# Fetching and weighing the other experts' rows inside the last expert's steps

## The reference

```python
def moe_swiglu(h, router_w, w1, w3, w2):
    t = h.reshape(-1, shp[-1])
    logits = (t @ router_w).astype(jnp.float32)
    top_v, top_i = lax.top_k(logits, TOP_K)                  # TOP_K = 2
    top_w = jax.nn.softmax(top_v, axis=-1)
    gates = jnp.sum(jax.nn.one_hot(top_i, N_EXPERTS) * top_w[..., None], axis=1)
    y = jnp.zeros_like(t)
    for e in range(N_EXPERTS):                               # 8 experts, 3584 wide
        y = y + gates[:, e:e + 1] * swiglu(t, w1[e], w3[e], w2[e])
...
x_lat = x_lat + ms[5] * rmsnorm(y_lat, post_ffn_g[l])
```

## Time and profile before

| | |
|---|---|
| median of three runs | 1730.58 us |
| the profiled execution, its own time | 1729.34 us |
| its span, first to last instruction | 1727.5 us |
| TensorE busy | 1694.0 us, 98% |
| DVE busy | 1405.9 us, 81% |
| ACT busy | 1095.6 us, 63% |
| POOL busy | 84.2 us, 5% |
| granted TensorE clock, mean | 0.999 |

### The profile page before, as it was taken

How to read it: one execution, slowest core, us unless ns; L and a number is a source line. 1 busy time by engine, 2 the same in 40 slices (tenths; PEclk the granted TensorE clock), 3 DMA queues, 4 the chain that set the end, 5 groups by cost and what they waited for, 6 DMA issues and landing times.

```text
span 1727.5 us, 24198 instructions
## 1 busy us (share of the span) xinstructions
PE 1694.0 (98%) x7988; PEld 1373.9 (80%) x7988; DVE 1405.9 (81%) x1625; ACT 1095.6 (63%) x1403; POOL 84.2 (5%) x97
## 2 busy tenths in 40 slices
PE   7999999999999999999999999999999999999997
PEld 4876878888788877787888888888888888888885
DVE  4947677375664589879999999999999999999998
ACT  5435462222222354777788888888888888888886
POOL 0114000000010010300100000000000000000001
PEclk9999999999999999999999999999999999999999
DMA  9858826264475358369999999999999999999995
GB/s 344 293 183 293 286 89 197 90 191 132 149 232 165 119 93 299 119 237 351 378 397 395 395 388 394 370 380 393 358 395 388 362 396 376 375 395 369 383 377 189
DMA packets 229696, 506.05 MB, mean 293 GB/s; under 512 B 16304, under 2 KB 47152, under 8 KB 229344
## 3 DMA queue, kind: packets, MB, share of 16 engines
q1 hardware_dynamic: 225296, 493.04, 80.0%
q0 software_dynamic: 4320, 12.00, 2.4%
HBM read 498.12 MB, written 19.96 MB: 300 GB/s over the span
## 4 chain that ended last, share of the span: by engine, by line
PE 92%; DVE 4%; issue 1%; ACT 1%; DMA 1%; SPq 0%; DVEq 0%; ACTq 0%
PE ps L661 29%; PE ps L663 28%; PE ps L662 28%; PE ps L1203 1%; DVE w_lo L1742 1%; PE ps L918 1%; PE ps L953 1%; DMA raw<-in_ada_w 1%; PE ps L941 0%; PE ps L688 0%; PE ps L1169 0%; PE ps L708 0%; PE ps L770 0%; DMA xs<-in_x 0%; PE ps L681 0%
## 5 line engine op out<-in xcount | busy, mean ns | idle before, releaser
L1742 DVE TENSOR_TENSOR w_lo<-raw,w_hi 128x1024 fp32r<-128x1024 f32 x570 | 684.1, 1224 | 163.7 <-ACT w_hi L1279 136.9
L1653 ACT ACTIVATE w_hi<-raw 128x1024 fp32r<-128x1024 f32 x448 | 473.0, 1061 | 103.0 <-PE ps L663 102.7
L661 PE MATMUL ps<-w_hi,he_hi 128*128 128x512 f32 x896 | 353.9, 395 | 0.7 <-DVE w_lo L1742 0.6
L663 PE MATMUL ps<-w_hi,he_lo 128*128 128x512 f32 x896 | 349.5, 390 | 0.0
L662 PE MATMUL ps<-w_lo,he_hi 128*128 128x512 f32 x896 | 348.9, 389 | 0.0
L1742 DVE TENSOR_TENSOR w_lo<-raw_more,w_hi 128x1024 fp32r<-128x1024 f32 x224 | 273.2, 1225 | 29.5 <-ACT w_hi L1653 12.0
L1653 ACT ACTIVATE w_hi<-raw_more 128x1024 fp32r<-128x1024 f32 x224 | 237.7, 1062 | 49.5 <-PE ps L663 49.5
L1279 ACT ACTIVATE w_hi<-raw 128x1024 fp32r<-128x1024 f32 x122 | 128.3, 1059 | 206.0 <-PE ps L663 185.4
L663 PEld LDWEIGHTS ps<-w_hi,he_lo 128*128 128x128 f32 x896 | 168.2, 188 | 35.8
L661 PEld LDWEIGHTS ps<-w_hi,he_hi 128*128 128x128 f32 x896 | 168.2, 188 | 35.3 <-DVE w_lo L1742 1.6
L662 PEld LDWEIGHTS ps<-w_lo,he_hi 128*128 128x128 f32 x896 | 168.4, 188 | 33.6
(11 more groups left out here) (304 smaller groups left out, 1956.4 us busy)
## 6 DMA issues: line engine op xcount, KB each, us to landing
raw<-in_moe_w SPq DMA_DIRECT2D x448, 512.0 KB, 6.4
raw_more<-in_moe_w SPq DMA_DIRECT2D x224, 512.0 KB, 6.5
raw<-in_ada_w SPq DMA_DIRECT2D x96, 512.0 KB, 4.8
raw<-in_ffn_w SPq DMA_DIRECT2D x66, 512.0 KB, 4.4
raw<-in_w_in SPq DMA_DIRECT2D x40, 512.0 KB, 6.6
raw<-in_w_out SPq DMA_DIRECT2D x16, 512.0 KB, 5.9
yrows<-in_x SPq DMA_DIRECT2D x9, 512.0 KB, 16.8
xe<-xrows SPq DMA_DIRECT2D x7, 512.0 KB, 6.6
```

Of the source, the lines that this page charges most:

```text
L661: pe.matmul(o, lh, rh, start=start, stop=False)
L663: return pe.matmul(o, ll, rh, start=False, stop=stop)
L1653: act.activation(w_hi[:, s % SPL, :], expert_raw(i), ACT.Copy).then_inc(hi_done, 1)
L1742: dve.tensor_tensor(w_lo[:, s_ % SPL, :], src, w_hi[:, s_ % SPL, :].bitcast(F32), ALU.subtract)\
```

## The change

Four things change.

- POOL no longer waits for the landing of unit 83 of the last expert but for that of unit 26 (`FETCH_AT`), then for `y kept`, and gathers the four pieces ahead of its branch. In the branch, if it is taken, it gathers them again.
- DVE weighs and sums one piece in each of steps 3 to 6 of the last expert (`SUM_STEP`), behind `ae32` and ahead of the next `w_lo`: (tb 0, j 0), (tb 0, j 1), (tb 1, j 0), (tb 1, j 1). Each waits for both gathers of its block, and DVE waits for its end before it goes on.
- Behind the branch the weighing is gone; in the branch it is done anew from the second gather.
- The four semaphores of the gathers become two, one for each block.

```diff
+FETCH_AT = 26
+SUM_STEP = 3
...
-            landed, count = expert_in(UE - 1)
+            def fetch_rows():
+
+                for tb in range(NLAT):
+                    for j in range(2):
+                        pool.indirect_dma_start(ygot[:, tb, j, :], None, yrows[:, :],
+                                                bass.IndirectOffsetOnAxis(ap=dest[:, NLAT * j + tb:NLAT * j + tb + 1], axis=0))\
+                            .then_inc(sg("y got%d" % tb), 16)
+
+            landed, count = expert_in(FETCH_AT)
             pool.wait_ge(landed, count + (NE - 1) * (16 * UE // RAW_E))
             pool.wait_ge(sg("y kept"), 16 * (NE - 1))
+            fetch_rows()
             with pool.If(busiest > P):
                 pool.wait_ge(sg("y kept"), 32 * NE)
-            for tb in range(NLAT):
-                for j in range(2):
...
+                fetch_rows()
...
+            def weigh_rows(tb, j, count):
+
+                dve.wait_ge(sg("y got%d" % tb), 2 * count)
+                gate = rs[:, 4 + 2 * j + tb:5 + 2 * j + tb]
+                if j == 0:
+                    ins = dve.tensor_scalar(yout[:, tb, :], ygot[:, tb, 0, :], gate, None, ALU.mult)
+                else:
+                    ins = dve.scalar_tensor_tensor(out=yout[:, tb, :], in0=ygot[:, tb, 1, :], scalar=gate, in1=yout[:, tb, :],
+                                                   op0=ALU.mult, op1=ALU.add)
+                ins.then_inc(sg("y summed"), 1)
+                dve.wait_ge(sg("y summed"), 4 * (count // 16 - 1) + 2 * tb + j + 1)
...
                         dve.tensor_tensor(ae32[:, s % 2, :], sge[:, s % 2, :], ps[:, 2 * (s % 2) + 1, :], ALU.mult)\
                             .then_inc(sg("ae32"), 1)
+                        if last and turn == 0 and s >= SUM_STEP:
+                            weigh_rows((s - SUM_STEP) // 2, (s - SUM_STEP) % 2, 16)
                         if s:
                             split_to(end_w2(s - 1) + AHEAD - (s == STEPS - 1))
...
             with dve.If(busiest[0] > P):
                 experts(1)
-            def sum_rows(tb):
...
+                for tb in range(NLAT):
+                    for j in range(2):
+                        weigh_rows(tb, j, 32)
...
-            sum_rows(0)
-            sum_rows(1)
             add_last(0)
             add_last(1)
```

More of the change, by code:

```diff
@@ L645, in _ @@
             busiest = pool.value_load(flag[0:1, 0:1], min_val=0, max_val=NLAT * P)
-            landed, count = expert_in(UE - 1)
+            def fetch_rows():
[5 more added lines that the diff above has]
+            landed, count = expert_in(FETCH_AT)
             pool.wait_ge(landed, count + (NE - 1) * (16 * UE // RAW_E))
             pool.wait_ge(sg("y kept"), 16 * (NE - 1))
+            fetch_rows()
             with pool.If(busiest > P):
                 pool.wait_ge(sg("y kept"), 32 * NE)
-            for tb in range(NLAT):
-                for j in range(2):
-                    pool.indirect_dma_start(ygot[:, tb, j, :], None, yrows[:, :],
-                                            bass.IndirectOffsetOnAxis(ap=dest[:, NLAT * j + tb:NLAT * j + tb + 1], axis=0))\
-                        .then_inc(sg("y got%d%d" % (tb, j)), 16)
+                fetch_rows()
         @block.tensor
```

## The result

| | kernel before | changed kernel |
|---|---|---|
| median, 20 runs each | 1729.32 us | 1732.13 us |
| from the lowest to the highest | 1728.62 to 1731.64 | 1730.08 to 1733.27 |
| the profiled execution, its own time | 1729.34 | 1732.18 |
| its span | 1727.5 | 1730.4 |

The ratio of the changed kernel to the one before is 1.0013, 95% interval 1.0007 to 1.0019. The median lies 0.7 us above the 1731.4 that was forecast, inside the range. The median of the kernel before, over 20 runs, is 1.3 us lower than the three runs had shown, so the difference of the medians is 2.8 us where 0.8 was forecast. It is smaller than the 0.2% (3.5 us) that the prediction asked of a measurement; but the interval lies wholly above 1, so with 20 runs of each kernel a small loss can be told.

The account below looks back on a forecast made before the run. TensorE was taken to set the pace. Span 1727.5 + 0.35 + 1.12 - 0.67 = 1728.3 us, 0.80 more; on the 1730.58 median that gives 1731.4 us, range 1728.8 to 1733.8.

Parts of the forecast that it names:

- The room of DVE: Last expert: weighing behind ae32 costs nothing in steps 3 and 5, 0.35 us in step 4, 1.12 in step 6.
- all hidden: Rival, 17%: in the last expert TensorE loses nothing and only the end's 0.67 us is won; 1729.9 us.
- less room: Rival, 12%: in the last expert all four weighing operations cost TensorE, 0.3 us more at each; 1732.6 us.
- The fetch costs nothing: Gather behind unit 26: weights land in at most 12.7 us, within the 14.5 allowed, so 0 us.
- The backlog: DMA queues behind the moved fetch: colliding transfers add 5.4 us to the 7.3 us landing of weights.
- starves the weights: Rival, 6%: the fetch makes ACT's w_hi 3.6 us late from about 1633 us, felt fully by TensorE; 1735.0 us.
- The exclusive lock: Shared DVE and GpSimd ports: a w_lo could stand still while POOL issues; as a rival 1%, 1735.6 us.
- The end gains 0.67 us: Behind the branch: without the weighing the fourth addition starts at 1718.07 instead of 1718.74, gaining 0.67 us.
- The sum: Whole kernel: losses of 0.35 and 1.12 us less the 0.67 gain, 0.80 us more; forecast 1731.4 us, 61%.

Follow-up runs that it names:

- sum_step2: Changed kernel with DVE's four weighing operations in steps 2 to 5 instead of 3 to 6; 1730.96 us, 1.0003 of the kernel before.
- double_mul: Changed kernel with each multiplication of steps 3 and 5 done twice; 1732.07 us, 1.0015 of the kernel before.
- fetch_only: Changed kernel with the fetch left at unit 26 but the weighing put back behind the branch; 1729.02 us, 0.9994 of the kernel before.
- fetch_twice: fetch_only with the rows gathered a second time once the first gather landed, 4 MB instead of 2; 1731.79 us, 1.0010 of the kernel before.
- before_again: The kernel before, unchanged, traced a second time; 1730.60 us, 1.0003 of the kernel before.
- after_again: The changed kernel, unchanged, run once more; 1730.71 us, 1.0005 of the kernel before.
- fetch_late: fetch_only with the fetch waiting for unit 83 again, as in the kernel before; 1729.44 us, 0.9997 of the kernel before.
- interleaved: Changed kernel weighing earlier in each step, ahead of ae_lo; block 0's mean square and half gate between the additions; 1729.01 us, 0.9998 of the kernel before.
- one_count: The kernel before with one semaphore for each block's gathers in place of two; 1730.37 us in one run.

## Why the prediction was right, and where it was not

*The room of DVE* held. The predicted places stall and the others do not: step 4 lost 0.35 us on the spot as predicted, step 6 1.10 where 1.12 was predicted, steps 3 and 5 nothing. The whole expert grew by 1.54 where 1.47 was predicted; the 0.07 left lie in the matmuls behind the wait of step 4, of which some are 0.24 apart instead of 0.23. sum_step2 and double_mul follow the same rule at other steps and at another size, within 0.1 us. The rival "all hidden" is out, and "less room" too: 0.35 us of slack is left at the multiplications.

*The fetch costs nothing* held, by fetch_only. Its working was less good. Unit 26, issued at 1615.15, took 9.0 us to land where 7.3 at most had been read the earlier trace rows; the landing there differs between executions (8.1 at most in fetch_only's). The backlog added 13.3 - 9.1 = 4.2 us to that and not 5.4. Both errors together left 1.2 us of margin in place of 1.8. The forecast of no cost was right all the same, and fetch_twice shows that the rival "starves the weights" was a true danger at twice the size.

Two pages of the Trainium skill were weighed there. In the changed kernel POOL issues its first gather from 1624.45 to 1626.00 while DVE makes four `w_lo`:

```profile
1622.71 5.15 DVE L1749 TENSOR_TENSOR w_lo<-raw,w_hi 128x1024 fp32r<-128x1024 f32 x4
```

The same four take 5.15 us in the kernel before, where POOL issues nothing at that place. The exclusive lock, as the prediction applied it to every issue of POOL, would have made one of them stand still; it did not. The Trainium skill's "SBUF — State Buffer" (Who interferes with whom) says less than that: an operation of DVE with two inputs in SBUF, as `w_lo` is, contends only with one of GpSimd that reads SBUF, and `tensor_tensor` was not seen to stall a DMA. With that the trace agrees. That each DMA engine takes turns between the queues (the Trainium skill, "DMA: Bandwidth & Descriptors", SWDGE vs HWDGE vs iDMA) fits the later landings, but no run here tells it from a queue that is simply longer.

*The end gains 0.67 us* is the step that failed. "The fourth addition starts now at 1718.74. Without the weighing it can start at 1718.03 + 0.04 = 1718.07" is right for the one execution that was profiled, and the changed kernel's trace seemed to confirm it with 13.49 against 14.15. But the 1718.74 rests on a 2.26 us branch wait that six of seven traces do not have. With 1.5 us DVE is through with the weighing 0.8 us earlier, and TensorE's `last_rows` already bounds the fourth addition: 4.81 us behind the last matmul in before_again, 4.81 in after_again. The third addition of before_again starts at 4.08 and DVE could go on 0.60 later, so the weighing was hidden there by some 0.1 us, and moving it wins nothing. In an execution like the first one the 0.67 us may be won; one trace has it, and how often it comes is not shown. The prediction had named the 2.26 us and asked only where they would end, not whether they would be there.

*The sum.* With the gain struck out the change costs (119.23 + 13.49) - (117.71 + 13.48) = 1.53 us, in place of 0.80. The spans of after_again and before_again, whose last experts start at 1595.21 and 1595.23, differ by the same: 1728.0 - 1726.5 = 1.5 us, or 0.09%. Both measured intervals hold that, 1.0007 to 1.0019 and 0.9996 to 1.0014. The fastest of the 20 executions of each kernel say the same, 1730.08 - 1728.62 = 1.46 us. So the change is a small loss, about twice the 0.80 us that were forecast. That the first median came within 0.7 us of the 1731.4 is in part luck: the three runs from which the forecast started had a median 1.3 us too high, and the medians lie 1.3 us further apart than the traces make the change; stretches of half clock (last section) could do that, but this is not shown. The ends of the range, too, are 0.1 and 0.2 us wider than the working beside them gives (1729.9 - 1.0 and 1732.6 + 1.0).

## What to carry to other kernels

Work of an engine that is not the bottleneck is free only at places where it is ahead: here the same 4.22 us of DVE cost TensorE 1.5 us behind `ae32` and 0.08 us a few instructions earlier, and the room of each place could be read to 0.1 us as the distance between the end of the producer and the start of its consumer. Before work is moved out of the end of a kernel, see whether the engine that waits there for another would be the later one in any case. A term that hangs on a single idle time put down to "issue" should be read from two traces of the same code before it enters a sum, and the DMA queues of that stretch looked at beside it.

## What the runs showed of the hardware

- *The way past a branch.* DVE's idle time over the skipped second run of the experts is 1.46 to 1.51 us in six traces and 2.26 in one, with the same code in two of them. DVE goes on 1.82 to 1.84 us behind the start of a packet of kind instruction in all seven.
- *Stretches at half the clock.* The 2.05 us by which the last expert starts later in the changed kernel's profile are not the change's: after_again starts it at 1595.21. Most of them, 1.6 us, arise in a stretch near 247 us, in layer 0. Columns as in the earlier trace rows, first the kernel before, then the changed one:

```profile
247.00:251.00 4.00, 4.00 (x18) 3.29 (x19) 3.83 (x11) 4.00 (x7) 0.00 (x0) 1.00 0.04 5
```

```profile
247.00:251.00 4.00, 3.87 (x10) 3.08 (x11) 3.84 (x10) 4.00 (x8) 0.00 (x0) 0.57 0.00 0
```

  The granted clock is 0.57 on the mean, for 3.41 us it is at 1.2 in place of 2.4 GHz, and TensorE works on 10 matmuls instead of 18. From the start of the first of them to that of the 22nd pass 6.5 us instead of 4.9. Just ahead TensorE was idle for 0.99 us, waiting for DVE's `hT_lo`; but it was so in traces without the drop too. It is in five of the thirteen traces (changed, fetch_late, fetch_twice, interleaved, one_count). Another drop near 21 us, of 6.83 us, is in three (fetch_only, sum_step2, fetch_twice): at 58 us they are 1.4 to 2.2 us behind the kernel before. In before_again and double_mul it lasts only 3.41 us there, and at 58 us they are 0.2 us ahead and 0.3 behind: it costs next to nothing. For the stretch from 20 to 30 us, the kernel before and then fetch_only:

```profile
20.00:30.00 10.00, 9.04 (x68) 5.56 (x68) 5.02 (x12) 3.52 (x7) 0.00 (x0) 1.00 1.09 356
```

```profile
20.00:30.00 10.00, 8.63 (x40) 4.90 (x41) 3.86 (x7) 2.78 (x5) 0.00 (x0) 0.66 1.09 355
```

  Of one and the same code some executions have such a drop and others have none: one such drop is as large as the effect of the change or larger. The times of the kernel before go with it: executions with a mean granted clock of 0.999 took 1728.4 to 1729.6 us, those with 0.995 took 1731.2 to 1732.3. What starts a drop stays open.
- *A backlog of DMAs.* With the DMA engines full, 2 MB more raised the landing of a piece of weights from 5.7 us (kernel before, issued 1622 to 1647) to a median of 12.4, and 4 MB to 16.4.
